# A norm by token halves behind its last two slabs, and the first modulation from TensorE tile by tile

## What is computed

```
mod = silu(c) @ ada_w + ada_b             # 9 vectors of 1024: (shift, scale, gate) x 3, for context and latent
x = x + 0.5*g1 * swiglu(rms(x)*nw[0]*(1+sc1) + sh1, ffn1)
x = x +     g2 * mixer (rms(x)*nw[1]*(1+sc2) + sh2)     # retention and HGRN2 branches, gates, w_o
x = x + 0.5*g3 * swiglu(rms(x)*nw[2]*(1+sc3) + sh3, ffn2)
y = rms(x) * final_norm_w
rms(x) = x * rsqrt(mean(x*x) + 1e-6)      # over the 1024 features of a token
swiglu(h) = (silu(h @ w1) * (h @ w3)) @ w2                # inner width 2816 = 22 tiles of 128
```

## Time and profile before

| what | us |
|---|---|
| median of the runs | 2042.55 |
| the profiled execution | 2041.4 |
| its span, first to last instruction | 2039.5 |
| TensorE matmul busy | 1923.0 (94%) |
| VectorE busy | 1006.1 (49%) |
| GpSimd busy | 807.7 (40%) |
| ScalarE busy | 511.3 (25%) |

### The profile page before, as it was taken

One profiled execution on the slowest core, in us unless ns is written; L12 is line 12 of the kernel. 1 busy time (PEld: TensorE's weight loads), 2 busy tenths in 40 slices (PEclk: granted clock), 3 DMA queues, 4 the chain that ended last, 5 costly groups with the idle time before them and its releaser, 6 DMA issues.

```text
span 2039.5 us, 33687 instructions
## 1 busy us (share of the span) xinstructions
PE 1923.0 (94%) x13036; PEld 1898.0 (93%) x13036; DVE 1006.1 (49%) x1458; ACT 511.3 (25%) x727; POOL 807.7 (40%) x436
## 2 busy tenths in 40 slices
PE   5898999999789999999999998999998999999997
PEld 4898999999689999999989998999997999999996
DVE  8776577476537888888851324210134221221123
ACT  2311001001146655566642213200114010100011
POOL 5355555566720000000032233445555555455455
PEclk8999999999899999999999999999998999999999
DMA  7343243334211111111121121112221122221222
GB/s 264 153 157 112 104 165 133 136 114 148 90 54 55 57 54 46 57 57 37 56 90 62 57 62 52 61 63 82 70 75 62 62 83 76 69 82 64 81 83 83
DMA packets 52484, 176.71 MB, mean 87 GB/s; under 512 B 6848, under 2 KB 9664, under 8 KB 52032
## 3 DMA queue, kind: packets, MB, share of 16 engines
q1 hardware_dynamic: 47952, 170.11, 23.8%
q10 hardware_dynamic: 4464, 5.64, 0.8%
HBM read 171.00 MB, written 4.72 MB: 86 GB/s over the span
## 4 chain that ended last, share of the span: by engine, by line
PE 82%; DVE 10%; issue 3%; ACT 2%; DMA 1%; DVEq 0%; SPq 0%; ACTq 0%
PE acc L335 74%; PE mix L927 4%; DVE ada_prod L425 2%; PE mix L1216 1%; PE mix L946 1%; DVE hg_bf L855 1%; DMA ada_raw<-ada_dram 1%; DVE hg_pb L855 1%; DVE hg_lo L1109 1%; PE mix L1200 1%; ACT L713 1%; PE mix L1211 0%; DVE w_lo L325 0%; PE mix L1224 0%; DVE hg_srun L892 0%
## 5 line engine op out<-in xcount | busy, mean ns | idle before, releaser
L311 POOL TENSOR_SCALAR w_hi<-raw 128x1024 fp32r<-128x1024 f32 x200 | 243.8, 1219 | 1178.7 <-PE acc L335 1085.2
L335 PE MATMUL acc<-h_hi,w_hi 128*128 128x320 f32 x2816 | 660.0, 316 | 52.1 <-DVE h_lo L529 31.5
L335 PE MATMUL acc<-h_hi,w_lo 128*128 128x320 f32 x2816 | 644.4, 310 | 0.0
L335 PE MATMUL acc<-h_lo,w_hi 128*128 128x320 f32 x2816 | 644.2, 310 | 0.0
L335 PEld LDWEIGHTS acc<-h_hi,w_hi 128*128 128x128 f32 x2816 | 470.9, 189 | 59.7 <-issue 52.8
L313 POOL TENSOR_TENSOR w_lo<-raw,w_hi 128x1024 fp32r<-128x1024 f32 x200 | 512.6, 2563 | 16.6
L335 PEld LDWEIGHTS acc<-h_lo,w_hi 128*128 128x128 f32 x2816 | 473.7, 189 | 0.0
L335 PEld LDWEIGHTS acc<-h_hi,w_lo 128*128 128x128 f32 x2816 | 473.1, 189 | 0.0
L425 DVE CUSTOM_DVE_ANT_0 ada_prod<-ada_raw,c_row 128x1024 f32<-128x1024 f32 x130 | 229.9, 1804 | 4.2 <-DMA ada_raw<-ada_dram 1.4
L540 DVE SCALAR_TENSOR_TENSOR x<-acc,mod,x 128x128 f32 x168 | 63.2, 432 | 239.5 <-PE acc L335 238.9
L335 PE MATMUL acc<-u_hi,w_hi 128*128 128x320 f32 x704 | 163.6, 314 | 13.1 <-DVE x L540 13.0
(11 more groups left out here) (214 smaller groups left out, 1910.0 us busy)
## 6 DMA issues: line engine op xcount, KB each, us to landing
raw<-w_dram SPq DMA_DIRECT2D x240, 512.0 KB, 3.7
ada_raw<-ada_dram SPq DMA_DIRECT2D x65, 512.0 KB, 5.4
ada_pe<-ada_pe_dram SPq DMA_DIRECT2D x7, 512.0 KB, 9.7
x<-x_dram SPq DMA_DIRECT2D x2, 1280.0 KB, 10.2
y_dram<-x SPq DMA_DIRECT2D x8, 320.0 KB, 2.4
c_row<-in_c_dram SPq DMA_DIRECT2D x1, 1024.0 KB, 5.1
hg_sin<-s_hg_dram ACTq DMA_DIRECT2D x8, 128.0 KB, 2.0
out_hg_dram<-hg_sfin ACTq DMA_DIRECT2D x8, 128.0 KB, 1.7
```

The costliest lines, as they stand in the source:

```text
L311: pool.tensor_scalar(w_hi[:, slot, :], raw[:, slot, :], 1.0, 1.0, ALU.mult, ALU.mult).then_inc(hi_done, 1)
L335: last = pe.matmul(acc[g][:, b, 0:HT], w[:, s, k * P:(k + 1) * P], tile[:, b * HT:(b + 1) * HT], start=(k == 0 and n == 0), stop=(k == k_t ...
```

## The change

Head: all 16 tiles of the first shift and scale are computed on TensorE (`HEAD_PE` 7 to 16), in pairs (`ada_pe_pair`): pair k holds shift tile k and scale tile k. SP loads `x` first, then the pairs, with the slabs of `up10` among them; VectorE turns each pair into coefficients (`head_coefs`). Pairs 4 to 7 stand between the products of the first two slabs. The sum of squares moves from GpSimd to VectorE. VectorE has 56 tiles left, four per step of `up1c`, three per step of `down10` and `down11`, none in `down12`. `FF_CHUNKS` becomes (6, 8, 8). In `up` VectorE's tiles stand behind `u_lo` of each half step, no longer ahead of `u_full`; in `down` one stands behind each of three residuals. The `down` phases use slots (0, 2, 1, 2). The small chain for the decays is cut into three pieces.

Norms 1 to 3: the last two slabs ahead are multiplied for tokens 0 to 319 first and for 320 to 639 then (`tail_halves`), and squares, sums, Newton step and tiles are done per half (`tail_dve`, `tail_act`); the next phase's first two slabs take half 0, then half 1 (`pair_halves`). The tile is scaled by `(x*scale)*rstd` on VectorE in one operation, ScalarE adds the shift and rounds.

```diff
-FF_CHUNKS = (8, 8, 6)
+FF_CHUNKS = (6, 8, 8)
-HEAD_DVE, HEAD_PE = 9, 7
+HEAD_PE = 2 * KT
...
-    ADA_PLAN += [(f"up1{_c}", _n // 2, 4), (f"down1{_c}", KT // 4, 2)]
+    ADA_PLAN += [(f"up1{_c}", _n // 2, 4)]
+    if _c < 2:
+        ADA_PLAN += [(f"down1{_c}", KT // 4, 3)]
...
-                   (f"down{_f}{_c}", KT // 4, (0, 1, 2, 1), (0, 1, 0, 1))]
+                   (f"down{_f}{_c}", KT // 4, (0, 2, 1, 2), (0, 1, 0, 1))]
...
-        def load_ada(sp, m, slot, before):
-            sp.wait_ge(ada_read, before + ADA_SLOTS)
+        def load_ada(sp, m, slot):
+            sp.wait_ge(ada_read, m + 2)
...
+        def tail_halves(pe, name, n, src_hi, src_lo, k_tiles, use):
+            i = KT // 4 - 1
+            for p in (2, 3):
...
+                for k in range(k_tiles):
+                    products(pe, name, p, k, src_hi, src_lo, k_tiles, banks=(0,))
+            for p in (2, 3):
+                for k in range(k_tiles):
+                    products(pe, name, p, k, src_hi, src_lo, k_tiles, banks=(1,))
+                    if p == 2 and k == k_tiles // 2:
+                        norm_pe(pe, n, 0, use)
...
+        def head_pe(pe):
+            ada_pe_pair(pe, 0)
+            ada_pe_pair(pe, 1)
+            norm_pe(pe, 0, None, Uses.norm1[1])
+            ada_pe_pair(pe, 2)
+            ada_pe_pair(pe, 3)
...
+            for k in range(KT):
+                pe.wait_ge(hlo_done, k + 1)
+                for p in range(2):
+                    products(pe, "up10", p, k, h_hi, h_lo)
+                if k + 4 < KT:
+                    ada_pe_pair(pe, k + 4)
...
+            scaled_dve(dve, n, 0, 0)
+            scaled_dve(dve, n, 1, 0)
+            square_add(dve, n, 6, 1)
+            tile_lo_dve(dve, n, 0, 0)
+            residual_tile(dve, name, STEP, 3, part, 1, n)
+            for k in range(2, KT):
+                scaled_dve(dve, n, k, 0)
+                tile_lo_dve(dve, n, k - 1, 0)
+            tile_lo_dve(dve, n, KT - 1, 0)
+            norm_newton_dve(dve, n, 1, use)
...
@@ def up_dve @@
-                    if f == 1:
-                        ada_step(dve, name, i, (pa, pb))
                     acc_read(dve, name, pa, i)
...
                                       ALU.subtract).then_inc(ulo_done, 1)
+                    if f == 1:
+                        ada_step(dve, name, i, (pa, pb))
...
@@ SP, a step of a feed-forward phase @@
-                            load_slab(sp, name, 0, i)
-                            load_slab(sp, name, 1, i)
-                            if f == 1:
+                            for p in range(4):
+                                load_slab(sp, name, p, i)
+                            if name in ADA.first:
                                 load_ada_step(sp, name, i)
-                            load_slab(sp, name, 2, i)
-                            load_slab(sp, name, 3, i)
```

More of the change, by code:

```diff
@@ L128, in __init__ @@
     def __init__(self):
-        self.first, self.loads, self.total = {}, {}, HEAD_DVE
-        loads = [len(range(s, HEAD_DVE, ADA_SLOTS)) for s in range(ADA_SLOTS)]
+        self.first, self.loads, self.total = {}, {}, 0
+        loads = [0] * ADA_SLOTS
         for name, steps, per in ADA_PLAN:
@@ L477, in square_clear @@
[L477 to L489 removed]
+        STEP = KT // 4 - 1
@@ L495, in norm_pe, with mean_square @@
                 pe.wait_ge(counter, value)
[L496 to L497 removed]
+                for half in ((0, 1) if b is None else (b,)):
+                    last = pe.matmul(mix[1][:, half, 0:HT], ones[:], tile[:, half * HT:(half + 1) * HT],
                                      start=(step == 0), stop=(step == 2))
             last.then_inc(sq_summed, 1)
[L501 to L505 removed]
+        def mean_square(b):
+            return mix_v[1] if b is None else mix_v[1][:, b, :]
@@ new lines, in shaped, with norm_rstd_act @@
+        def shaped(tile, b):
+            return halves(tile[:]) if b is None else tile[:, span(b)]
+        def norm_rstd_act(act, n, b=None):
+            at = NORM[n, b]
+            act.wait_ge(sq_summed, at + 1)
+            act.activation(shaped(log_ms, b), mean_square(b), ACT.Ln, bias=eps[:, 0:1], scale=1.0 / D_MODEL).then_inc(log_done, 1)
+            act.wait_ge(log_done, at + 1)
+            act.activation(rstd[:, span(b)], log_ms[:, span(b)], ACT.Exp, scale=-0.5).then_inc(rstd_done, 1)
@@ new lines, in final_dve, with residual_tile @@
+        def final_dve(dve, k, b):
+            dve.scalar_tensor_tensor(out=x[:, k, span(b)], in0=x[:, k, span(b)], scalar=small["final_w"][:, k:k + 1],
+                                     in1=rstd[:, span(b)], op0=ALU.mult, op1=ALU.mult).then_inc(xn_done, 1)
+        def residual_tile(dve, name, i, p, part, b=None, n=0):
+            g = ST.phase[name][2][p]
+            tile = i * 4 + p
+            if b == 0:
+                dve.wait_ge(half_done, 2 * (n - 1) + p - 1)
+            else:
+                projected(dve, name, p, i)
+            for lo, hi, e in {None: ((0, CTX, 0), (CTX, HT, 1), (HT, T, 1))}.get(b) or segments(b):
+                src = acc[g][:, lo // HT, lo % HT:lo % HT + hi - lo]
+                last = dve.scalar_tensor_tensor(out=x[:, tile, lo:hi], in0=src, scalar=mod[:, part, tile, e:e + 1],
+                                                in1=x[:, tile, lo:hi], op0=ALU.mult, op1=ALU.add)
+            last.then_inc(half_evac if b == 0 else evacuated[g], 1)
@@ L583, in ff_pe @@
             for i in range(KT // 4):
-                for p in range(4):
+                for p in range(2 if c == 2 and i == STEP else 4):
                     project(pe, name, p, i, u_hi, u_lo, FF_CHUNKS[c],
                             tiles_done=(ulo_done, base + 1) if i == p == 0 else None)
+            if c == 2:
+                tail_halves(pe, name, 2 * f - 1, u_hi, u_lo, FF_CHUNKS[c], use)
         def u_base(f, c):
```

489 lines of the change are left out of this document (284 added, 205 removed).

## The result

The changed kernel took **2076.46 us** (median of 4 runs, 2073.97 to 2079.05) against 2042.35 (2041.32 to 2042.76) beside it: ratio 1.0169, 95% interval 1.0153 to 1.0184. The prediction was 2049 in a range of 2024 to 2068: the sign was right, the size was not. The profiled execution took 2076.35, its span was 2074.6 (before: 2039.5), so 35.1 us have to be found.

The account below looks back on a forecast made before the run. TensorE, busy 94%, was taken to bound the kernel, so only its standing or half-clock time could give. Terms +17 + 16.5 - 14.5 - 8 - 4 = +7 took 2041.4 to 2048.4, said as 2049, range 2024 to 2068.

Parts of the forecast that it names:

- Head, +17: Start to end of the first two `up10` slabs: eight pairs on TensorE, mostly at half clock, end it 17 us later.
- the rule of the clock that I weighed: Head: the skill's rule that TensorE activity releases the throttle; eight unbroken pairs would run at the upper level, ending at 65.1.
- The 2.5 us for a pair that meets the upper clock: Head, pairs among the first two slabs' products: 2.5 us taken off the 40.8 counted for four groups of products and pair.
- Steps of `up1`, +16.5: `up1`: SP's wait for the step's first modulation tile delays the next slab; TensorE stands 1.5 us in 11 steps.
- Rival B: `up1`: the slab lands soon enough, the step wait costs 0 to 0.2, total 2034; chance 0.17.
- Rival D: `up1`: the eleven short gaps drop the clock each time, 11 x 2.7 = +30, total 2079; chance 0.05.
- Residual waits, -14.5: `down10` and `down12`: of 19.7 us in residual waits and half clock, most goes, 4.2 stays in `down10`; bounds -8 and -19.7.
- 12.6 + 1.2 + 1.1: `down10`: first residual ends 14.9 us after `up10`, from the old 12.6, gate and small operations 1.2, half a residual pair 1.1.
- Norms, -8: Norms 1 and 2: halves win 7.1 and 4.8 us, less 4 for clock lost in the gaps; bounds -3 and -14.
- 2 for GpSimd, which splits a slab from 5.3 and another from 8.9: Norms 1 and 2: 2 us allowed for GpSimd's splits on the way to the first tile, put at 11.1.
- Rival E: Norms 1 and 2: halves win nothing because VectorE is the chain there, +8, total 2057; chance 0.11.
- End, -4: Last product to the end of the kernel: halves shorten 17.4 us to 13.3; bounds -2 and -5.

Follow-up runs that it names:

- 3: Changed kernel with pairs 4 to 7 of the first modulation contracted over one of eight input tiles only: 2047.24 us, ratio 1.0028.
- 4: Changed kernel with all eight pairs ahead of the first product, none among the products: 2073.1 us, ratio 1.0146.
- 7: Changed kernel with the first modulation shared: tiles 0 to 3 of shift and scale on TensorE, 4 to 7 on VectorE: 2056.24 us, ratio 1.0074.
- 1: Changed kernel with the fourth modulation tile of an `up1` step no longer waiting for the first tile of its own step: 2055.67 us, ratio 1.0065.
- 2: Changed kernel with exact slot waits: a phase's first slabs wait for the last slab that really used the slot: 2071.81 us, ratio 1.0132.
- 11: Changed kernel with exact slot waits, halves kept, third split behind norms 1 and 2 held until four tiles of half 0 are written: 2070.68 us, ratio 1.0146.
- 13: Changed kernel with the two-input subtraction of GpSimd's split replaced by two one-input operations, low part of weights left out: 2045.52 us, ratio 1.0009.

## Why the prediction came out as it did

**Head, +17: right** (+18.5). The price of a pair from one row, 6.96, held for seven of the eight (pair 2 was counted at 5.0), also at the end of 38 us without a pause. Experiments 3, 4 and 7 say that TensorE sets this end. That is what the rule of the clock that I weighed would have got wrong; the row decided. The closeness is part luck. The 2.5 us for a pair that meets the upper clock didn't come (granted 0.50 from 34 to past 88) and the first product came 1.0 early; in experiment 1 two pairs did meet it and the head ended 7.5 earlier.

**Steps of `up1`, +16.5: right** (18.3, and 20.8 came back in 1). The sum of five pieces gave 1.5 a step and 1.2 to 2.4 were measured. Rival B is out: no step was free. Rival D is out for this execution: the clock stayed up behind the short waits (14.36 us for 96 matmuls behind the one at 107.81, 0.150 each). It isn't out as a mechanism: in 2 the clock fell behind three of eleven.

**Residual waits, -14.5: a term mis-sized.** It came out at -9.7 (8.6 less 18.3), inside its bounds. The mechanism was right: one large wait in `down10`, none in `down12`. What failed was the step "12.6 + 1.2 + 1.1", which puts the end of the first residual 14.9 behind the end of `up10` and the wait at 2.8. Slab 2 started 18.0 behind it (166.05 to 184.09), and the wait was 5.88. In the trace after, the four products take
```profile
168.93 3.41 DVE L477 CUSTOM_DVE_ANT_0 ada_prod<-ada_raw,c_row 128x1024 f32<-128x1024 f32 x1
172.27 2.05 DVE L477 CUSTOM_DVE_ANT_0 ada_prod<-ada_raw,c_row 128x1024 f32<-128x1024 f32 x1
174.36 3.29 DVE L477 CUSTOM_DVE_ANT_0 ada_prod<-ada_raw,c_row 128x1024 f32<-128x1024 f32 x1
177.58 1.21 DVE L477 CUSTOM_DVE_ANT_0 ada_prod<-ada_raw,c_row 128x1024 f32<-128x1024 f32 x1
...
179.82 2.33 DVE L820 TENSOR_TENSOR soft<-in_lb 128x16 f32<-128x16 f32 x1
```
10.0, and an operation on 16 elements 2.33 in place of the 0.17 of its neighbours, all but the fourth product beside splits. I took the small operations from their lengths with GpSimd idle: from the last product to the first residual it was 4.1, where 0.9 + 1.2 was counted. The products I had inside the 12.6, and there they were stretched already, two of the four:
```profile
496.49 2.06 DVE L425 CUSTOM_DVE_ANT_0 ada_prod<-ada_raw,c_row 128x1024 f32<-128x1024 f32 x1
...
498.60 3.31 DVE L425 CUSTOM_DVE_ANT_0 ada_prod<-ada_raw,c_row 128x1024 f32<-128x1024 f32 x1
```
Those four took 7.8, the new ones 10.0, and `u_lo` was shorter by 1.2 (1.09 against 2.33). So 2.2 + 2.0 - 1.2 = 3.0 of the 3.1 is how the splits fell, and the earlier trace rows showed neither of the two long products. The rest of the term, about 2, isn't placed; by the same row of 14.36 each step wait costs about 0.2 beyond its length (96 matmuls at 0.1473 are 14.14), 2.4 in all, an estimate that 1 supports with its 20.8.

**Norms, -8: wrong, by the most** (+8.4, a miss of 16). Two steps failed. First, "2 for GpSimd, which splits a slab from 5.3 and another from 8.9": there were three splits back to back from 571.87 to 582.7, since `slot_clear` makes the first slab wait for one too late, and in norm 1 they cost VectorE 2.9 in the Newton step (1.27 and 2.56 where 0.49 is usual) and over 5 in the first `x_norm`. The first tile came 17.6 behind half 0's last product, not 11.1. In norm 2 the same late splits hit elsewhere: the Newton step was free of them (0.49 each), but TensorE waited 4.00 for the split itself, and 1.78 more for `h_lo` behind operations of 3.16 and 3.63:
```profile
1580.74 2.34 POOL L318 TENSOR_TENSOR w_lo<-raw,w_hi 128x1024 fp32r<-128x1024 f32 x1
```
Exact waits gave much of that back (2: norm 1 5.7 less, norm 2 2.4 less). Second, the gain itself: even with the splits placed well the halves took 42.7 and 44.2, the whole norm 43.2 and 43.1, the kernel before 45.1 and 42.8. Half as many tokens make the first tile earlier, and then TensorE stands within and between the halves (the three waits in 11). Rival E (the halves win nothing because VectorE is the chain) was the right one, given 0.11; the true case was worse than it, because splits take from VectorE what the halves ask of it.

**End, -4: right** (-4.4). There are no splits behind `down22`, so the same halving wins where GpSimd is silent. That this is the reason is argued, not shown: no run has the last norm whole, and its sums and its tile operation changed with it.

**Not in the sum:** +2.4 in the mixer and +1.6 in the second feed-forward. 0.7 of it is a wait for the split at 2050.78, as the one at 562.75: in the halved tails slab 3 stands in slot 2 behind slab 1. (The other two such waits lie in the norms' stretches.) The rest was not followed up.

In numbers: 1.5 + 1.8 + 4.8 + 16.4 + 4.0 - 0.4 = 28 us between the +7 forecast and the +35 of the spans. Head, steps and residual waits stayed inside their bounds; the norms' bound, -3, was off by 11 and the mixer and the second feed-forward had none. VectorE beside the splits stands behind two of the misses: a cause shared by two terms must widen both.

**What stays open:** how much of the 24 to 31 us that 13 gave back belongs to which stretch, since it also changed the splits' times in every phase; whether 11 gains over 2; and why a pair or a short wait meets the upper clock in one execution and not in another.

## What to carry to other kernels

Before an elementwise chain is priced, lay the other engine's rows of the same microseconds beside it: in these traces an operation of VectorE with two inputs in SBUF cost its own time plus most of the GpSimd operation it met (1.22 became up to 3.41), so take the stretched row where a split can fall, and put long GpSimd pieces where VectorE waits anyway. In an in-order load queue look for the wait that refers to work of the same step, and count the whole loop behind it. Halving a chain paid at the end of the kernel (-4.4) and not in the two norms where engines hand tiles on (42.7 and 44.2 at best, against 43.2 and 43.1 whole).

## What the runs showed of the hardware

GpSimd and VectorE took turns, instruction by instruction. A product of 1.22 took 3.41 beside a 2.4 us split and 2.06 beside a 1.05 one, and GpSimd's own pieces went from 1.05 to 2.02 and from 2.4 to 3.39. An operation of VectorE with one operand in PSUM was not held: `x<-acc,mod,x` took 0.55 at 575.88 beside GpSimd, as long as elsewhere, and the 44 `u_full`, which read `acc` too, all took 0.82. The Trainium skill (SBUF — State Buffer, "Terms") says that the two share a pair of ports, that the lock is exclusive and "held for the full instruction", and (GPSIMD Engine Reference, "Specifications") that instructions of VectorE with two SBUF inputs contend. By that rule the operations with two SBUF inputs stretch and the one with a PSUM input doesn't; the trace agrees with 3.41 against 0.55.

Fp32 matmuls with two columns let the clock fall and didn't bring it back: in 4 it was granted 1.00 for the first 3 us behind the norm's matmuls (0.11 us each) and 0.50 from 36 to the end at 69.5 (0.205 each). At the start of the run the column of the granted clock misleads. Windows of the changed kernel, columns as in the earlier trace rows:
```profile
12.00:16.00 4.00, 4.00 (x21) 1.00 1.03 418
34.00:38.00 4.00, 4.00 (x21) 0.50 1.06 354
```
The same matmuls, as many in 4 us, under 1.00 and under 0.50; and the norm's eight matmuls at 25.3 took 4.61, where they take 2.31 in the earlier trace rows. Up to about 30 the lengths say the lower level, as the prediction read them, though the column falls only near 34.
